# Summing modulation products as columns, and a second projection job in the first pass of a decoder layer

## The reference

```python
mod = silu(c) @ w_ada + b_ada            # six parts of 2048
shift1, scale1, gate1, shift2, scale2, gate2 = split(mod, 6)
u = x * (1 + scale1) + shift1
(cb, cc, ch, gq, gk, gv, gz, gb, ga, fq, fk, fv, ff, ma, mb, mc) = split(u @ w_in)
y_a = cb * conv3(cc * ch)                # the short convolution
y_b = gated_delta_rule(gq, gk, gv, gz, gb, ga)
y_c = forgetting_attention(fq, fk, fv, ff)
merged = sigmoid(ma)*(y_a @ w_a) + sigmoid(mb)*(y_b @ w_b) + sigmoid(mc)*(y_c @ w_c)
x = layer_norm(alpha * x + gate1 * (merged @ w_o))
x = layer_norm(alpha * x + gate2 * (relu(u2 @ w_ff1)**2 @ w_ff2))
```

## Time and profile before

| | |
|---|---|
| median of three runs | 2599.48 us (2598.27 to 2600.35) |
| profiled execution | 2600.64 us, span 2598.9 us |
| PE busy | 2539.2 us, 98% |
| DVE, ACT busy | 1728.9 us (67%), 1179.3 us (45%) |
| granted TensorE clock, mean | 0.986 |
| DMA queue of the weights | 522.29 MB, 64.8% of the engines' span |

### The profile page before, as it was taken

The page is one execution under the profiler, slowest core; times in us unless marked ns, Lnnn a source line. Parts: engine busy times, 40 slices in busy tenths (PEclk is TensorE's granted clock), DMA queues, the critical chain, the costliest instruction groups (busy, mean ns, idle before and its releaser), DMA issues.

```text
span 2598.9 us, 33407 instructions
## 1 busy us (share of the span) xinstructions
PE 2539.2 (98%) x12104; PEld 2071.6 (80%) x12104; DVE 1728.9 (67%) x2330; ACT 1179.3 (45%) x1477; POOL 85.3 (3%) x89
## 2 busy tenths in 40 slices
PE   7889999999999999999999999999999999999998
PEld 3567888788878887788788888888888888888886
DVE  4677767786578758776666777776765555546556
ACT  2146354635463445535444444434554444453442
POOL 0001010101001100100000000000000000000000
PEclk8799999999999999999999999999999999999999
DMA  9865657656665567555788787887656765666664
GB/s 317 307 201 169 180 171 226 182 175 180 196 215 169 158 201 235 172 154 170 230 267 256 254 264 237 266 257 259 189 170 194 227 185 189 193 184 194 189 185 148
DMA packets 300464, 540.05 MB, mean 208 GB/s; under 512 B 39185, under 2 KB 44817, under 8 KB 299281
## 3 DMA queue, kind: packets, MB, share of 16 engines
q1 hardware_dynamic: 271040, 522.29, 64.8%
q10 hardware_dynamic: 29264, 15.68, 2.0%
HBM read 534.68 MB, written 3.21 MB: 207 GB/s over the span
## 4 chain that ended last, share of the span: by engine, by line
PE 47%; DVE 2%; DMA 1%; issue 0%; ACT 0%; DVEq 0%; SPq 0%; ACTq 0%
PE acc L1798 47%; PE bank L1801 1%; DVE w_lo L1148 1%; DMA raw<-in_w_ff 0%; DMA raw<-in_w_o 0%; DVE z_lo L1132 0%; DVE xr L1138 0%; ACT zw_hi L665 0%; DVE zw_lo L1148 0%; DVE xr L1132 0%; DVE x L1138 0%; DVE xr L1666 0%; DVE ff_part L1760 0%; ACT w_hi L665 0%; DVE macc L1138 0%
## 5 line engine op out<-in xcount | busy, mean ns | idle before, releaser
L1148 DVE TENSOR_TENSOR w_lo<-raw,w_hi 128x1024 fp32r<-128x1024 f32 x788 | 967.2, 1227 | 650.9 <-ACT w_hi L665 606.1
L665 ACT ACTIVATE w_hi<-raw 128x1024 fp32r<-128x1024 f32 x780 | 822.4, 1059 | 1093.2 <-PE acc L1798 761.2
L1798 PE MATMUL acc<-w_hi,u_hi 128*128 128x512 f32 x2272 | 908.6, 400 | 22.3 <-DVE w_lo L1148 21.3
L1798 PE MATMUL acc<-w_hi,u_lo 128*128 128x512 f32 x2272 | 890.2, 392 | 0.0
L1798 PE MATMUL acc<-w_lo,u_hi 128*128 128x512 f32 x2272 | 889.9, 392 | 0.0
L1798 PEld LDWEIGHTS acc<-w_hi,u_hi 128*128 128x128 f32 x2272 | 429.4, 189 | 119.9 <-DVE w_lo L1148 25.5
L1798 PEld LDWEIGHTS acc<-w_hi,u_lo 128*128 128x128 f32 x2272 | 429.3, 189 | 91.6
L1798 PEld LDWEIGHTS acc<-w_lo,u_hi 128*128 128x128 f32 x2272 | 430.0, 189 | 85.2 <-issue 1.0
L1798 PE MATMUL acc<-w_hi,z_hi 128*128 128x512 f32 x880 | 344.0, 391 | 0.2 <-DVE w_lo L1148 0.2
L1798 PE MATMUL acc<-w_hi,z_lo 128*128 128x512 f32 x880 | 342.6, 389 | 0.0
L1798 PE MATMUL acc<-w_lo,z_hi 128*128 128x512 f32 x880 | 342.5, 389 | 0.0
(11 more groups left out here) (266 smaller groups left out, 1568.8 us busy)
## 6 DMA issues: line engine op xcount, KB each, us to landing
raw<-in_w_in SPq DMA_DIRECT2D x416, 512.0 KB, 4.5
raw<-in_w_ff SPq DMA_DIRECT2D x256, 512.0 KB, 4.3
raw<-in_w_ada SPq DMA_DIRECT2D x192, 512.0 KB, 4.8
raw<-in_w_branch_a SPq DMA_DIRECT2D x32, 512.0 KB, 4.9
raw<-in_w_branch_b SPq DMA_DIRECT2D x32, 512.0 KB, 4.9
raw<-in_w_branch_c SPq DMA_DIRECT2D x32, 512.0 KB, 5.1
raw<-in_w_o SPq DMA_DIRECT2D x32, 512.0 KB, 4.9
IT<-decay_d ACTq DMA_DIRECT2D x8, 512.0 KB, 7.6
```

What stands on the lines that cost most here:

```text
L665: a.activation(weights(n)[0], raw[:, rl % RAWS, :, :], ACT.Copy).then_inc(hi_ready.sem, 1)
L1148: v.tensor_tensor(lo, raw[:, rl % RAWS, :, :] if src is None else src, hi, ALU.subtract).then_inc(lo_ready.sem, 1)
L1798: return t_.matmul(dst, lhsT, rhs, start=start, stop=stop)
```

## The change

- **Columns.** For an odd k-tile PE now takes the load as weights, in four blocks of 128 columns, and streams one column of c: four matmuls, each of which leaves 128 sums as a column in bank 1. `first_sums(n, j, count)` gives load j of job n its own four places there, so nothing accumulates in PSUM. `first_columns` keeps only the four matmuls for `macc`. The row tile, ACT's `row_copy` and its waits are gone. `first_u` reduces the columns of each of two jobs with one DVE instruction.
- **A second job.** In the first stage 16 units are done instead of 8, GQ and CC: GQ units 0 to 5 in the first three groups as before, then CC units 0 to 5 between the last closing columns and `first_job(3)`, there GQ 6 and 7, and at the end CC 6 and 7. Pass 0 then runs in `FIRST_ORDER`; `place_of` gives the job's place and its `acc`. ACT copies CC into `early` (where x was) and the piece that turned CC out of `stage` takes it from there.
- **Side work.** In pass 0 `late` moves every `to(slot)` up to AT_CH by 16, and those from AT_CH on to two slots before the end and after. The modulation loads of pass 0 stand behind other units (`FIRST_MOD_AFTER`).

The core of the diff:

```diff
+FIRST_ORDER = (J_GQ, J_CC, J_GK, J_GV, J_GZ, J_FQ, J_FK, J_FV, J_CH, J_CB)
+FIRST_UNITS = 2 * UPJ
+FIRST_FILL = 6
+FIRST_MOD_AFTER = (18, 19, 20, 21, 22, 27, 28, 29) + tuple(u + UPJ for u in MOD_AFTER[UPJ:])
...
-    for u in range(FIRST_W):
-        yield "w", FIRST_W * (FIRST_GROUPS - 1) + u, 0
+    for u in range(FIRST_FILL, FIRST_UNITS):
+        yield "w", u, 0
+
+def first_work(n):
+    if n < FIRST_FILL:
+        return J_GQ, n
+    if n < 2 * FIRST_FILL:
+        return J_CC, n - FIRST_FILL
+    return (J_GQ, J_CC)[(n - 2 * FIRST_FILL) // 2], FIRST_FILL + n % 2
+
+FIRST_HI = (0, 1), (2, 3), (4, 5, 6, 7, 8), (9, 10, 11, 12, 13, 14, 15)
...
+def late(i, slot):
+    if i or slot >= SLOTS:
+        return slot
+    return slot + KT if slot < AT_CH else SLOTS - 2 + slot - AT_CH
...
+        def first_sums(n, j, count):
+            at = KT + (n * (UPJ + 1) + j) * BPC
+            return bank[1][:, at:at + count * BPC]
...
-            def row_copy(n):
-                act.wait_ge(N["raw_summed"].sem, pe_units(n, UPJ - 1))
-                if n >= 2:
-                    act.wait_ge(N["mcol_summed"].sem, n - 1)
-                activate(row_sb[0:1, n % 2, :], acc[1][0:1, n % 2, :], ACT.Copy, "row_in", n + 1)
...
                 take_job(i, J_GQ, stage[:, :, :])
                 if i == 0:
+                    take_job(i, J_CC, early[:, :, :])
...
-                tt(mod[:, k:k + BPC], b[:, KT:KT + BPC], bada[:, k:k + BPC], ALU.add)
+                for n in (2 * group, 2 * group + 1):
+                    sums = first_sums(n, 0, pe_count(n) + 1).rearrange("p (j b) -> p b j", b=BPC)
+                    o.do(v.tensor_reduce(mcol[:, n % 2, :], sums, mybir.AxisListType.X, ALU.add))
+                o.after()
+                tt(mod[:, k:k + BPC], mcol[:, 0, :], bada[:, k:k + BPC], ALU.add)
...
-                mm(acc[1][0:1, n % 2, :], c_act[:, k:k + 1], tile[:, 1, :], m == 0, m == UPJ - 1).then_inc(N["raw_summed"].sem, 1)
+                col = first_sums(n, pe_units(n, m) - pe_units(n, -1) - 1, 1)
+                for b in range(BPC):
+                    last = mm(col[:, b:b + 1], tile[:, 1, b * P:(b + 1) * P], c_act[:, k:k + 1])
+                last.then_inc(N["raw_summed"].sem, 1)
...
                 for b in range(BPC):
-                    col = bank[1 - n // 2 % 2][:, at + b:at + b + 1]
-                    mm(col, macc[:, n % 2, b * P:(b + 1) * P], ones[:, 0:1], True, False)
-                    last = mm(col, row_sb[0:1, n % 2, b * P:(b + 1) * P], ones[0:1, 0:1], False, True)
+                    last = mm(col[:, b:b + 1], macc[:, n % 2, b * P:(b + 1) * P], ones[:, 0:1])
...
             first_columns(NMOD_FIRST - 1)
+            for n in range(FIRST_FILL, 2 * FIRST_FILL):
+                fill(n)
             first_job(FIRST_GROUPS - 1)
+            for n in range(2 * FIRST_FILL + 2, FIRST_UNITS):
+                fill(n)
```

More of the change, by code:

```diff
@@ L142, in pe_units, with pe_count, place_of, mod_after @@
     return sum(on_pe(*divmod(v, UPJ)) for v in range(n * UPJ + m + 1))
+def pe_count(n):
+    return pe_units(n, UPJ - 1) - pe_units(n, -1)
 def first_chunk(n):
     return n // 2 + n % 2 * NCH
[L150 to L157, removed]
+def place_of(i, job):
+    return job if i else FIRST_ORDER.index(job)
+def late(i, slot):
+    if i or slot >= SLOTS:
+        return slot
+    return slot + KT if slot < AT_CH else SLOTS - 2 + slot - AT_CH
+def mod_after(i, u):
+    after = MOD_AFTER if i else FIRST_MOD_AFTER
+    return after.index(u) if u in after else None
+def raw_place(i, u):
+    return u + sum(mod_after(i, v) is not None for v in range(min(u, MAIN_UNITS)))
 def merge_mod_after(u):
@@ L523, in _ @@
                 else:
-                    load_first(r, w_in_t, UK * n, MAIN_JOBS[0])
+                    job, k = first_work(n)
+                    load_first(r, w_in_t, UK * k, MAIN_JOBS[job])
             for i in range(NCH):
[L526 to L532, removed]
+                r = 0 if i else FIRST_UNITS
+                for u in range(r, MAIN_UNITS):
+                    job = u // UPJ if i else FIRST_ORDER[u // UPJ]
+                    load(i * MAIN_RAW + (R_MAIN + r), r, w_in_t, UK * (u % UPJ), i * NC + MAIN_JOBS[job])
                     r += 1
@@ L737, in _ @@
                     activate(u_hi[:, 2 * g:2 * g + 2, :], uT[:, 2 * g:2 * g + 2, :], ACT.Copy, "u_hi_made", g + 1)
-                for u in range(FIRST_W * group, FIRST_W * (group + 1)):
+                for u in FIRST_HI[group]:
                     first_hi(u)
-                if group < FIRST_GROUPS - 1:
-                    row_copy(2 * group + 2)
-                    row_copy(2 * group + 3)
             o.end()
@@ L746, in _ @@
                 o.begin(i, 90)
-                count = [0 if i else UK * (UPJ - LEAD)]
+                count = [0 if i else UK * (FIRST_UNITS - LEAD)]
                 next_slot = slots(i, MAIN_UNITS, 0, MAIN_RAW, R_MAIN, raw_place, count)
@@ L753, in to @@
                 def to(slot):
[L754 removed]
+                    while count[0] < late(i, slot):
                         next_slot()
                 def take_job(i, job, dst, func=ACT.Copy):
[L759 to L761 removed]
+                    at = place_of(i, job)
+                    job_wait(act, i * len(MAIN_JOBS) + at)
+                    o.do_count(a.activation(dst, acc[at % 2][:, :, :], func),
+                               acc_free[at % 2].sem, i * (len(MAIN_JOBS) // 2) + (at // 2 + 2))
                 def take_last(i):
@@ L1171, in one @@
                         u = s // 2 + LEAD
-                        rl = place(u)
+                        rl = place(i, u)
                         lo_unit(i * units + (unit0 + u), u, rl)
-                        m = mod_after(u) if place is raw_place and u < MAIN_UNITS else None
+                        m = mod_after(i, u) if place is raw_place and u < MAIN_UNITS else None
                         if place is merge_place:
@@ L1354, in to @@
                 def to(slot):
-                    while count[0] < slot:
+                    while count[0] < late(i, slot):
                         next_slot()
@@ L1922, in first_job @@
                     pe.wait_ge(N["u_lo_made"].sem, g + 1)
-                    first_slot(UK)
+                    fill(g if group < FIRST_GROUPS - 1 else 2 * FIRST_FILL + g % 2)
             pe.wait_ge(N["masks_made"].sem, 1)
@@ L1961, in _ @@
             for i in range(NCH):
-                count = first_count if i == 0 else [0]
+                count = [0 if i else FIRST_UNITS * UK]
                 next_slot = slots(i, MAIN_UNITS, 0, count, lambda job, s: (u_hi, u_lo))
@@ L1987, in to @@
                 def to(slot):
-                    assert count[0] <= slot, (count[0], slot)
-                    next_slot(slot - count[0])
+                    assert count[0] <= late(i, slot), (count[0], slot)
+                    next_slot(late(i, slot) - count[0])
                 def turn_last(i):
@@ L2167, in _ @@
                 wait("yc_made", 1)
[L2168 removed]
+                turn_stage(0, "c_turned", 1, stage if i else early)
                 to(AT_CH)
```

57 lines of the change are left out of this document (23 added, 34 removed).

## The result

Median 2613.44 us (2606.82 to 2616.14, 6 runs) against 2599.91 us (2598.27 to 2603.25, 6 runs) of the kernel before beside it: ratio 1.0046, interval 1.0034 to 1.0059. The change costs 13.5 us. The direction was forecast, the size was not: 30.5 us had been expected, and the time lies just under the range worked out term by term, 2615 to 2645 us, and near the lower end of the one stated last, 2608 to 2645 us. The profiled execution took 2613.74 us, its span is 2611.9 us.

The account below looks back on a forecast made before the run. PE's own order was taken to bound each round, with loads keeping up. Terms (a) to (d) net +29.7 us and (e) +1 gave +30.7 us, a median of 2630 us; range 2615 to 2645, finally 2608 to 2645.

Parts of the forecast that it names:

- What bounds the kernel: First-pass rounds: PE's own order fills the round, loads keep up; PE busy 27.49 of 30.82 us.
- (a): Sums of a first-pass round: 13 column groups, mostly at the lower clock, 24.5 us; a round +8.5, two rounds +17.0 us.
- (b): Start of the first pass: column groups and transposes at the lower clock make the first `first_job` end 10.5 us late.
- (c): Last two jobs before `first_job(3)`: 11 column groups take 20.4 us instead of 15.4, +5.0 us.
- (d): Fill ending the first pass: ten units hide the u chain, 32.7 us; eight units (22.6 us) then missing from pass 0.
- (e): Pass 0 side work 16 k-tiles on: modulation loads crowd DVE near the small logarithms; +1 us, bounds -3 to +6.
- Rival 1: First-pass column runs: the clock stays up, so columns cost no more than before; 2598 us, 8% chance.
- Rival 2: First-pass columns: much cheaper than priced because loads are drawn ahead, so loads set the round; 2586 us, 4% chance.
- Rival 3: First-pass rounds: the clock goes up and down, half of (a) to (c) is paid; about 2614 us, 6% chance.

Follow-up runs that it names:

- the sets: The kernel before with the closing sums as four macc columns, then four row columns, each in its own PSUM place, without accumulation: 2592.38 us, ratio 0.9963.
- the columns alone: The kernel before with the column sums only, no second job in the first stage, side work where it was: 2614.51 us, ratio 1.0043.
- the row sums with GQ held back: The changed kernel with row sums, modulation loads two units earlier, each group's two GQ units behind the next group's closing sums: 2585.44 us, ratio 0.9937.

## Why the direction was right and the size was not

**What bounds the kernel: right.** PE's order fills each round, the loads keep up (DMA share 0.84 in the rounds; below 0.8 had been forecast), and the loss is busy time of PE.

**(a) The columns: mechanism and place right, price wrong.** The forecast let 2.7 groups of a round run at the upper level and 10.3 at the lower. That is what happened: the thirteen groups took 20.08 us (64.96 to 85.04), which at 0.88 and 1.71 us a group is 2.6 groups at the upper level. What failed is the price of a group, 1.24 and 2.06 us, where 0.88 and 1.71 us were measured. It was four times 0.31 and 0.51 us, the steps of the closing columns, in which 128-row and 1-row weights alternate; the sets showed that the alternation itself costs. In place of the forecast's 24.5 us, 2.7 x 0.88 + 10.3 x 1.71 = 20.0. `first_job` was 0.9 us shorter than taken (86.37 to 98.96 is 12.59, not 13.45), since the clock came back sooner in its first unit. A round thus grew by 3.1 us, not 8.5: two rounds +6.2, forecast +17.0. The reason given, that no row sums are left to raise the clock, is too simple: with a row sum behind every load it fell all the same (0.51 from 87.68 to 115.63).

**(b) The start: the same term.** `first_job(0)` ended at 64.96, 4.7 us late, forecast 10.5. The last closing columns ended near 51.1 instead of 56.0, because the ten groups took 16.3 us (1.63 each), not 20.6, and the nine sets of transposes 8.0, not 9.0; and `first_job(0)` took 12.3 us, not 13.45.

**(c) The last two jobs:** 16.27 us instead of 15.45, +0.8, forecast +5.0. By the measured prices 2.7 x 0.88 + 8.3 x 1.71 = 16.6.

**(d) The fill: right.** Ten units took 30.74 us without a wait, forecast 32.7; the eight units that are then missing from pass 0 were worth 21.75 us, forecast 22.6, because 2.83 us was the step of a unit in the closing part, not in the passes. With row sums in place of columns the first stage was ahead by 6.0 us, 2.2 of them because the last closing sums ended earlier (1.7 by the clock that did not fall in the first round); 3.8 are the fill's, forecast 2.8.

**(e) Side work: +5.1 us behind the first turning, forecast +1, bounds -3 to +6.** 1.6 us were lost up to the next turning, round the longer wait in the stretch of the logarithms, as the working feared; with the earlier modulation loads that stretch took 1.1 us less than before, and only 0.4 us were lost behind the first turning in all. At CH's turning no new crowd was seen: the first pass's last turning stood 10.2 us late, no worse than its middle. 0.8 us more came up to FQ's turning and 2.8 in the passes 1 to 3 and the merge, whose instructions the change doesn't touch; the columns alone, which move nothing, lose 3.6 us behind the first turning, and the row sums with GQ held back gain 2.4. The cause of these was not settled.

**The sum with one price changed.** By the forecast's own steps with 0.88 and 1.71 us: (a) 20.0 + 1.01 + 0.3 + 13.45 = 34.8, +4.0 a round; (b) 26.4 + 17.1 + 9.0 + 1.3 + 13.45 = 67.2, +7; (c) +1.2; last column at 153.6; (d) 186.3, +36.0 less 22.6 = +13.4; (e) +1: about 2614 us on the median, where 2613.4 was measured. That it comes so near is partly luck: by parts the first turning came 5.5 us earlier than this sum has it (+7.9, not +13.4), and what follows lost 4.1 us more (+5.1, not +1).

**The rivals.** Rival 1, the clock stays up, asked for 1.00 in the odd jobs; it read 0.50. By the Trainium skill, "TensorE: Matmul & The Clock Gate", section "Why this matters for your kernels", a TensorE kept busy without longer idle gaps should hold the upper clock; the trace disagrees again, with 11.95 us of uninterrupted columns at 0.50. Rival 2, much cheaper columns, was right in that the forecast's price was too high: 0.88 us a load at 1.00, not 1.24. It was wrong on what follows from it, since the clock doubles that price for most of a round. Rival 3, half way, gave 2614 us and was hit by the number; its reason, a clock that goes up and down within the round, was not what happened.
The Trainium skill, same page, section "LDWEIGHTS (loading the stationary operand)", puts a load of 128 columns at 107 ns; eight loads, an estimate from that page, are 0.85 us a group. At the upper level a group takes 0.88 us (79.14 to 80.02, above), which agrees, although single records of a load read 188 ns. At the lower level a group takes 1.71 us, which that section doesn't tell.

## What to carry to other kernels

Price an operation from a run in which it stands among its own kind: a step taken between two kinds of matmul holds the change-over as well. Before PE's work is given another form, look at which clock the present form gets and price both forms at both levels; here columns and row sums cost the same per load at either level, and all of the loss lay in the level. And a wait at the head of a round is best filled with work that is already there: holding back two units gave more than either part of the change.

## What was not expected of the hardware

- Eight f32 columns with 128-row and 1-row weights in turn took 2.48 us, and 1.96 us in two sets of four; writing to the same PSUM place or to another made no difference.
- Behind the alternating columns seven row sums took 7.79 us with the clock at 0.50 for part of them, behind the sets 6.10 us at 1.00, in both rounds of each run; but in the first round of the run with row sums and the second job they took 6.10 us behind alternating columns too.
- One row sum behind every four columns did not hold the clock (0.51 from 87.68 to 115.63); one matmul with 128 weight columns behind them held it at 1.00 in the first round and in the last two jobs and lost it within the second round, with the same kind of work. Row sums among themselves had come back to 1.00 in the kernel before (101.30 to 104.94).
